# Expert output stage of a four-layer block: the twelve products of a tile ordered by halves over four PSUM banks, the lower weights last and behind a wait of their own

## The reference, cut to what matters

```python
def block(args):
    hx, ix, gx = args
    u_sel = jnp.take(peer_u, ix, axis=0)
    v_sel = jnp.take(peer_v, ix, axis=0)
    act = jax.nn.gelu(jnp.einsum('td,ted->te', hx, u_sel), approximate=False)
    return jnp.einsum('te,ted->td', gx * act, v_sel)
```

## Time and profile before

| | |
|---|---|
| median of three runs | 4401.1 us (4397.94 to 4401.52) |
| the profiled execution's own time | 4403.54 us |
| its span from first to last instruction | 4401.4 us |
| TensorE matmul busy | 4103.0 us, 93% |
| VectorE busy | 3083.8 us, 70% |
| ScalarE busy | 2417.5 us, 55% |
| mean granted TensorE clock | 0.975 |

### The profile page before, as it was taken

One profiled execution on the slowest core, in us unless ns is written; L12 is line 12 of the kernel. 1 busy time (PEld: TensorE's weight loads), 2 busy tenths in 40 slices (PEclk: granted clock), 3 DMA queues, 4 the chain that ended last, 5 costly groups with the idle time before them and its releaser, 6 DMA issues.

```text
span 4401.4 us, 84718 instructions
## 1 busy us (share of the span) xinstructions
PE 4103.0 (93%) x30226; PEld 3722.4 (85%) x30226; DVE 3083.8 (70%) x5135; ACT 2417.5 (55%) x4061; POOL 95.5 (2%) x182
## 2 busy tenths in 40 slices
PE   6899997899999999789998999969999999987999
PEld 6899997777899999767788999957777799986777
DVE  6758858777565786787756688597775578768555
ACT  4146658544533665754446566574444466566444
POOL 0000000000000000000000000000000000000000
PEclk9999999999998999999998999999998899999999
DMA  7345551687514555258843555418883255531564
GB/s 272 109 134 176 177 181 57 198 283 253 166 54 130 169 176 180 81 164 283 264 154 117 176 176 179 158 38 281 283 284 121 77 167 177 180 125 62 191 191 156
DMA packets 203623, 748.63 MB, mean 170 GB/s; under 512 B 22704, under 2 KB 23856, under 8 KB 202192
## 3 DMA queue, kind: packets, MB, share of 16 engines
q1 hardware_dynamic: 178416, 646.51, 44.3%
q0 software_dynamic: 25056, 100.15, 7.5%
HBM read 745.52 MB, written 1.05 MB: 170 GB/s over the span
## 4 chain that ended last, share of the span: by engine, by line
PE 82%; DVE 10%; issue 3%; ACT 3%; DMA 1%; DVEq 1%; POOL 0%; SPq 0%; ACTq 0%; POOLq 0%
PE ps L1916 14%; PE ps L1917 14%; PE ps L1918 14%; PE ps L2365 11%; PE ps L2367 11%; PE ps L2366 11%; DVE t_lo L1760 3%; PE ps L2063 2%; DVE oh L1768 2%; DVE arena L1779 2%; DVE t_lo L1105 1%; PE ps L1932 1%; PE ps L2319 1%; PE ps L2210 1%; ACT t_hi L627 1%
## 5 line engine op out<-in xcount | busy, mean ns | idle before, releaser
L1105 DVE TENSOR_TENSOR t_lo<-raw,t_hi 128x1024 fp32r<-128x1024 f32 x1180 | 1445.2, 1225 | 1074.9 <-ACT t_hi L627 1050.9
L627 ACT CAST t_hi<-raw 128x1024 fp32r<-128x1024 f32 x1180 | 1237.7, 1049 | 1574.3 <-PE ps L1918 800.0
L1916 PE MATMUL ps<-h_hi,t_hi 128*128 128x256 f32 x5344 | 1549.0, 290 | 45.1 <-DVE h_lo L1227 19.1
L1917 PE MATMUL ps<-h_lo,t_hi 128*128 128x256 f32 x5344 | 1525.5, 285 | 0.0
L1918 PE MATMUL ps<-h_hi,t_lo 128*128 128x256 f32 x5344 | 1524.6, 285 | 0.0
L1916 PEld LDWEIGHTS ps<-h_hi,t_hi 128*128 128x128 f32 x5344 | 1038.0, 194 | 68.5 <-issue 44.5
L1917 PEld LDWEIGHTS ps<-h_lo,t_hi 128*128 128x128 f32 x5344 | 1040.2, 195 | 0.8 <-issue 0.5
L1918 PEld LDWEIGHTS ps<-h_hi,t_lo 128*128 128x128 f32 x5344 | 1039.0, 194 | 0.0
L2365 PE MATMUL ps<-t_hi,h_hi 128*128 128x512 f32 x2048 | 816.4, 399 | 19.9 <-DVE t_lo L1105 10.6
L2367 PE MATMUL ps<-t_hi,h_lo 128*128 128x512 f32 x2048 | 803.3, 392 | 0.0
L2366 PE MATMUL ps<-t_lo,h_hi 128*128 128x512 f32 x2048 | 801.8, 391 | 0.0
(11 more groups left out here) (279 smaller groups left out, 2894.9 us busy)
## 6 DMA issues: line engine op xcount, KB each, us to landing
raw<-u_tiles SPq DMA_DIRECT2D x512, 512.0 KB, 3.3
raw<-v_tiles SPq DMA_DIRECT2D x512, 512.0 KB, 4.2
raw<-w_tiles SPq DMA_DIRECT2D x188, 512.0 KB, 3.6
oh<-w_tiles POOLq DMA_DIRECT2D x160, 512.0 KB, 4.8
arena<-w_tiles SPq DMA_DIRECT2D x16, 512.0 KB, 3.7
arena<-keys_t POOLq DMA_DIRECT2D x4, 1024.0 KB, 5.0
arena<-mla_w POOLq DMA_DIRECT2D x1, 4096.0 KB, 14.7
arena<-lora POOLq DMA_DIRECT2D x2, 1280.0 KB, 8.6
```

What stands on the lines that cost most here:

```text
L627: act.copy(t_hi[:, j % SPL, :], raw[:, j % RAW, :]).then_inc(hi_done, 1)
L1105: tts(t_lo[:, j % SPL, :], raw[:, j % RAW, :], t_hi[:, j % SPL, :].bitcast(F32), ALU.subtract).then_inc(lo_done, 1)
L1916: mm(o, hi[:, c, :], h_hi[:, c, :], start=(c == 0), stop=False)
L1917: mm(o, hi[:, c, :], h_lo[:, c, :], start=False, stop=False)
```

## The change

The body of `step` in segment `v` of all four layers is written in another order. The same twelve matmuls stand there, with the same operands, into the same banks. First come the four upper-by-upper products, one for each bank, then the four with the lower activations, then the four with the lower table part. The wait at the head of the tile is for `hi_done` instead of `lo_done`; the wait for `lo_done` stands ahead of the ninth matmul. `tile_used` is raised by the twelfth as before. Inside a bank the order of two of the three products swaps.

```diff
                 def step(n, j, k, i):
-                    pe.wait_ge(lo_done, n + 1)
+                    pe.wait_ge(hi_done, n + 1)
                     pe.wait_ge(wal, k + (1 + KEYS * l))
                     b = j % 4
                     one, last = (i is None and k == 0), (i is None and k == KEYS - 1)
-                    for tt in range(TT):
-                        up = wa_hi[:, b, tt * P:(tt + 1) * P]
-                        down = wa_lo[:, b, tt * P:(tt + 1) * P]
-                        for half in range(2):
-                            cols = slice(half * 512, (half + 1) * 512)
-                            o = ps[:, 2 + 2 * tt + half, :]
-                            mm(o, up, t_hi[:, j % SPL, cols], start=one, stop=False)
-                            mm(o, up, t_lo[:, j % SPL, cols], start=False, stop=False)
-                            ins = mm(o, down, t_hi[:, j % SPL, cols], start=False, stop=last)
+                    parts = [(tt, half, slice(half * 512, (half + 1) * 512)) for tt in range(TT) for half in range(2)]
+                    for tt, half, cols in parts:
+                        mm(ps[:, 2 + 2 * tt + half, :], wa_hi[:, b, tt * P:(tt + 1) * P], t_hi[:, j % SPL, cols],
+                           start=one, stop=False)
+                    for tt, half, cols in parts:
+                        mm(ps[:, 2 + 2 * tt + half, :], wa_lo[:, b, tt * P:(tt + 1) * P], t_hi[:, j % SPL, cols],
+                           start=False, stop=False)
+                    pe.wait_ge(lo_done, n + 1)
+                    for tt, half, cols in parts:
+                        ins = mm(ps[:, 2 + 2 * tt + half, :], wa_hi[:, b, tt * P:(tt + 1) * P], t_lo[:, j % SPL, cols],
+                                 start=False, stop=last)
                     ins.then_inc(tile_used, 1)
```

## The result

The changed kernel takes 4362.6 us (median of four runs, 4358.1 to 4365.9) against 4401.3 us: ratio 0.9912, interval [0.9898, 0.9926]. Beside other kernels on another chip it took 4367.7 us against 4400.7, ratio 0.9924 [0.9909, 0.9939]. It is faster, by 39 us on the first chip and 33 on the second. I had added up 27.9 us and forecast 4375, with a range from 4365 to 4397. The direction and the mechanism hold, the size was too small.

A forecast was written before the change was run, and what follows sets the result against it. TensorE, busy for 93% of the span, was taken to set the pace. Late starts 18, filled pauses 5.5 and clock 4.4 summed to 27.9 us off the profiled 4403.5, giving 4375.6, stated as 4375 us, range 4365 to 4397.

The forecast's parts named there:

- The new wait: Wait for `lo_done` ahead of the ninth matmul, 512 in all: taken as 0, with 72 us as upper bound.
- Bank order: Visiting the banks in turn three times per tile: taken as 0, bound +-6 us over 6144 matmuls.
- the rival that hoped for 0.213: Alternating banks removes 0.0134 us from each of 6144 matmul steps: 82 us more won, 4293 us; 3 in 100.
- the clock rival: Short pauses from going round the banks lower TensorE's clock: 123 us over one tile in ten (4500); 1 in 100.
- The gain does not arrive: Tiles not landed by DMA, or lateness from elsewhere, leave mostly the gain at stage starts: 4388 to 4398 us; 10 in 100.
- I take 18 as given back, since some of the 23 will be jitter of the DMA and rest: Late tile starts inside the loops of the `v` stages: 18 us gained of 23 us counted as lost.
- the second count: Late starts counted from timeline rows: 0.2 us per four tiles, 19 us in layers 0 to 2, 1 to 2 in layer 3.
- The starts: Second tile of layers 0 to 2: 5.5 us from filled pauses and 4.4 us from the clock after them.
- the clock term: Less low clock after the start pauses: 1.6 us each in layers 0 and 1, half of 2.4 in layer 2; 4.4 us.

The follow-up runs named there:

- start_head: The changed kernel with tile 1 written out ahead of the loop and tiles 0 and 1 waiting for `lo_done` at their head: 4380.6 us, 0.9956 of the kernel before.
- loop_head: The changed kernel with tile 1 written out and tiles 2 to 127 waiting for `lo_done` at their head: 4394.7 us, 0.9985 of the kernel before.
- wait_each: The changed kernel with a wait of its own ahead of each of a tile's twelve products: 4368.5 us, 0.9913 of the kernel before.
- order_only: The changed kernel's product order, with the wait for `lo_done` back at the tile's head and none in mid-tile: 4399.95 us, 0.9992 of the kernel before.
- by_banks: The changed kernel with the first eight products bank by bank, two in a row into the same bank: 4367.5 us, 0.9914 of the kernel before.
- fold_later: The changed kernel with pieces L1208 and L1210 of the next layer's modulation one tile later on VectorE: 4365.6 us, 0.9916 of the kernel before.
- head_wait_rest: The changed kernel with the late wait only in tile 0 of each stage, all others waiting for `lo_done` at their head: 4401.0 us, 1.0002 of the kernel before.

## Why the prediction fell short

*What bounds, and the mechanism: right.* TensorE set the pace, `t_lo` was the late operand, and both places that I named (heads inside the loop, second tile of layers 0 to 2) gave what the change won. `start_head` and `loop_head` show each by itself.

*"The new wait. [...] I take 0": right.* `wait_each` shows it with ten more. *"Bank order. [...] it costs and gives 0": right*, by `order_only` and `by_banks`. The steps read in the earlier trace rows were enough for that. The step of 0.227 us stays in all kernels, and so the rival that hoped for 0.213 is out; the clock rival too, with a granted clock of 1.00 in the stages. The 215.8 ns that the prediction takes from the Trainium skill ("TensorE: Matmul & The Clock Gate", section "Back-to-back issue gap") are given there for a matmul by itself. For a stream of pairs of weight load and matmul, which this kernel is, the same section has about 131 ns at 512 columns. This case's 226.7 ns agree with neither.

*"The gain does not arrive": out.* The stages run at 2.72 us a tile with DMA busy for 0.80, 0.80 and 0.86 of its time in layers 0 to 2, so the tiles do land in time. (Its times, 4388 to 4398, lack the 2.4 us between profile and median; nothing hangs on it.)

*"I take 18 as given back, since some of the 23 will be jitter of the DMA and rest": the failed step.* The term measured 22.6 us. From the third tile on the tiles of the changed kernel take 2.72 us, so nothing of the 23 was jitter; by the experiments, `loop_head` gives 20 to 24 back. The discount had no row behind it, and the second count did not carry it either: 19 and 1 to 2 for layer 3 are 20 to 21. That count was itself short. It put 0.03 us on the tile that starts at 2110.67, from the length of its first matmul, where the tile lost 0.06; four tiles lose 0.22. And it gave layer 3 1 to 2 us, where it lost 2.8, 0.02 us a tile, with `t_lo` 0.2 to 0.3 us ahead of every start.

*The starts: 9.9 forecast, 11.7 found.* I had 5.5 for the filled pauses and 4.4 for the clock. By the tiles' lengths the pauses gave about 6.0 (10.8 us before, 4.8 after) and the clock 5.7 (7.3 before, 1.6 after). The clock gave more than I took because tile 1 ran at full clock in all three layers, also in layer 2. The new pauses came out at 1.84, 1.48 and 0.60 us idle where I had 1.0, 1.1 and 3.3. Layer 2 is so short for two reasons: its first tile now fell under the lower clock (four L2361 in 1.86 us) and ran 1.6 us longer, which covered part of the wait, and `t_lo` of tile 1 was ready 7.0 us after the stage's start and not 7.9 as before. This moment moves with the DMA that L1208 waits for. The lower clock moves too: in layer 0 the first tile had it before (granted clock 0.60 from 799.9 to 803.0) and not after, in layer 2 after and not before, so that 1.6 us came and went without the change. In the repeat of the change the pause of layer 0 was 3.36 us and tile 2 still had the lower clock behind it. So the clock term is an average, not a fixed return.

*A term that was missing: the stages the change doesn't touch.* Span less `v` stages is 2965.2 us in the profile before and 2961.3 after. In `order_only` it is 2962.6, in `wait_each` 2959.5, in `fold_later` 2968.7, in the repeat of the change 2969.4 and in `head_wait_rest` 2952.9: 16.5 us apart for the same code. Of the 16.5 us, 11.2 lie between the `v` stages of layers 2 and 3: 711.9 us at a granted clock of 0.97 in `head_wait_rest`, 723.1 at 0.96 in the repeat. The mean granted clock of the whole goes with it. The summary rows of `head_wait_rest` and of the repeat of the change:

```profile
core 0: 4384.6 us, clock 0.980
```

```profile
core 0: 4374.5 us, clock 0.977
```

With levels of 1.2 and 2.4 GHz a mean of 0.980 is 2 x 0.020 x 4384.6 = 175 us at the lower one, 0.977 is 201 us. If such a stretch is full of matmuls, it loses half its length, so 26 us more are an estimate of 13 us of time, near the 16.5 seen. No run held the clock fixed, so this is argued and not shown. My range came from the stages alone and left this scatter out. Of the 10.3 us that I was short in the profile 3.9 are of this kind, 4.6 the loop, 1.8 the starts. The number 4375 holds a slip as well: 4375.6 less the 2.4 us to the median is 4373.2. With 34.3 in place of 27.9 it is 4366.8, inside the range: that the first time fell out of it at 4362.6, and the second stayed in at 4367.7, lies within this scatter.

## What to carry to other kernels

When an operand is split in parts that are made one after the other, put the products that need only the first part ahead and give the last part its own wait: that is worth the lateness at each head, and nothing where another producer is the late one, as the `u` stage showed. Read the time of an undisturbed tile from the trace, and take the whole difference to the stage's length as what a removed wait can give; discount it only by rows that name another cause. When you count what late starts cost, measure from one tile's start to the next one's: the length of its first matmul shows only part of it. A range for a change of under 1% has to hold the scatter of the stages that are not changed, which here was 16 us between profiles.

## What the runs showed of the hardware

A wait on a matmul that is met ahead of time is free here, even twelve per tile. That is 1402.0 us of stages against 1401.9. A head wait that is met only just ahead is not: with `t_lo` 0.37 us ahead of the tile's start nothing was lost, with 0.20 it was 0.06 us, and the late one, where the matmul started 0.13 us behind `t_lo`, lost 0.14. In layer 3, with 0.2 to 0.3 us, it was 0.02 us a tile on average. The first weight load of a tile starts 0.22 us ahead of its matmul when the wait is met early, and 0.01 us ahead when it is met late. Four fp32r matmuls of 512 columns take 0.91 us whatever the banks, 0.227 each, where 512 columns at 2.4 GHz are 0.213.
